# Three feed-forward stages: up products in Strassen's form, with the activations kept in DRAM

## The reference, cut to what matters

```python
# block 1 (FF = 4096) and block 3 (FF = 4096), with other names
m = rmsnorm(h, g) @ w_up            # (1024 x 1024) @ (1024 x 4096)
h = h + square(relu(m)) @ w_down    # (1024 x 4096) @ (4096 x 1024)
# block 2 (FF = 2816)
h = rmsnorm(x, g)
x = x + (silu(h @ w_gate) * (h @ w_up)) @ w_down
```

## Time and profile before

| | |
|---|---|
| median of 3 runs | 4399.23 us |
| span of the profiled execution (first to last instruction) | 4393.7 us |
| difference between the two | 5.5 us |
| TensorE busy (matmul) | 3927.2 us, 89% |
| VectorE busy | 2089.7 us, 48% |
| ScalarE busy | 1119.0 us, 25% |
| GpSimd busy | 869.4 us, 20% |
| DMA, mean | 73 GB/s, 319.75 MB |

### The profile page before, as it was taken

The page is one execution under the profiler, slowest core; times in us unless marked ns, Lnnn a source line. Parts: engine busy times, 40 slices in busy tenths (PEclk is TensorE's granted clock), DMA queues, the critical chain, the costliest instruction groups (busy, mean ns, idle before and its releaser), DMA issues. The chain is left out here.

```text
span 4393.7 us, 47463 instructions
## 1 busy us (share of the span) xinstructions
PE 3927.2 (89%) x18690; PEld 3275.1 (75%) x18690; DVE 2089.7 (48%) x2012; ACT 1119.0 (25%) x1368; POOL 869.4 (20%) x653
## 2 busy tenths in 40 slices
PE   9965999999989986767999999999943979999997
PEld 8953888888878776655888888878733958888886
DVE  3677445254544556365331322444768545253353
ACT  2503200000222233244211111243154552000001
POOL 1110222222222210200222222222220512222221
PEclk9987999999999998878999999999967989999998
DMA  3310111111133322442111111122272531111111
GB/s 131 103 45 23 46 51 49 48 48 48 48 130 110 117 80 46 120 156 67 46 50 48 48 48 48 48 82 91 88 177 39 158 126 48 48 48 48 48 50 60
DMA packets 446784, 319.75 MB, mean 73 GB/s; under 512 B 100181, under 2 KB 411989, under 8 KB 446649
## 3 DMA queue, kind: packets, MB, share of 16 engines
q1 hardware_dynamic: 437288, 283.72, 22.0%
q10 hardware_dynamic: 9360, 34.21, 2.0%
HBM read 245.22 MB, written 72.66 MB: 72 GB/s over the span
## 5 line engine op out<-in xcount | busy, mean ns | idle before, releaser
L191 POOL TENSOR_TENSOR c_wlo<-c_raw,c_whi 128x1024 fp32r<-128x1024 f32 (+1 forms) x169 | 409.4, 2423 | 1457.9 <-ACT c_whi L185 1457.9
L220 PE MATMUL c_acc<-c_hi,c_whi 128*128 128x512 f32 x1616 | 633.6, 392 | 0.6 <-POOL c_wlo L191 0.6
L221 PE MATMUL c_acc<-c_lo,c_whi 128*128 128x512 f32 x1616 | 629.2, 389 | 0.0
L222 PE MATMUL c_acc<-c_hi,c_wlo 128*128 128x512 f32 x1616 | 629.2, 389 | 0.0
L191 POOL TENSOR_TENSOR w_wlo<-w_raw,w_whi 128x1024 fp32r<-128x1024 f32 x116 | 291.6, 2514 | 1163.6 <-ACT w_whi L185 1163.6
L220 PE MATMUL c_acc<-pair,c_whi 128*128 128x512 f32 x1120 | 438.1, 391 | 45.6 <-POOL c_wlo L191 45.6
L185 ACT ACTIVATE c_whi<-c_raw 128x1024 fp32r<-128x1024 f32 (+1 forms) x169 | 177.1, 1048 | 1112.5 <-PE c_acc L222 1109.3
L221 PE MATMUL c_acc<-pair,c_whi 128*128 128x512 f32 x1120 | 437.5, 391 | 0.0
L222 PE MATMUL c_acc<-pair,c_wlo 128*128 128x512 f32 x1120 | 437.4, 391 | 0.0
L220 PE MATMUL c_acc<-c_hi,w_whi 128*128 128x512 f32 x1024 | 405.5, 396 | 12.4 <-POOL w_wlo L191 12.4
L221 PE MATMUL c_acc<-c_lo,w_whi 128*128 128x512 f32 x1024 | 399.7, 390 | 0.0
(11 more groups left out here) (592 smaller groups left out, 5858.7 us busy)
## 6 DMA issues: line engine op xcount, KB each, us to landing
c_raw<-in_w_ff SPq DMA_DIRECT2D x64, 512.0 KB, 4.0
proj<-c_tot ACTq DMA_DIRECT2D x49, 512.0 KB, 2.6
w_raw<-in_w_in SPq DMA_DIRECT2D x48, 512.0 KB, 4.4
c_raw<-in_w_gu SPq DMA_DIRECT2D x44, 512.0 KB, 3.8
w_raw<-in_w_mlp_up SPq DMA_DIRECT2D x32, 512.0 KB, 4.0
w_raw<-in_w_mlp_down SPq DMA_DIRECT2D x32, 512.0 KB, 4.0
h<-proj SPq DMA_DIRECT2D x25, 512.0 KB, 5.7
c_raw<-in_w_in SPq DMA_DIRECT2D x25, 512.0 KB, 4.0
```

The costliest lines, as they stand in the source:

```text
L191: pool.tensor_tensor(s.wlo[b][:, 0:kt, :], raw[:, 0:kt, :], s.whi[b][:, 0:kt, :].bitcast(F32), ALU.subtract).then_inc(s.lo[b], 1)
L220: pe.matmul(out, s.whi[b][:, k, :], x_hi, start=(k == 0), stop=False)
L221: pe.matmul(out, s.whi[b][:, k, :], x_lo, start=False, stop=False)
L222: mm = pe.matmul(out, s.wlo[b][:, k, :], x_hi, start=False, stop=(k == kt - 1))
```

## The change

Each pair of up tiles (256 columns of `w_up`; in block 2 one gate tile and one up tile) is seen as a 2x2 block product and computed in the form of Strassen and Winograd: the token axis is cut in two halves, the 256 columns in two, and the inner dimension in even and odd k (4 each). The pair takes seven products of half size, each 4 (k) x 3 = 12 matmuls of 512 columns, in place of eight.

- The sums of weights are made by GpSimd (`sums`: four operations of 512 elements per pair). The lower parts of the weights are made by VectorE (`split` there: three of 1024 elements, one of 512), the upper ones by ScalarE.
- The sums of activations are made once per stage: `E` for products 0 to 3, and `u4`, `u5` for 4 to 6. Some are made while the projection still runs, the others while the first pair does.
- Products 0, 3 and 6 accumulate in the same bank. ScalarE copies what is in PSUM to SBUF between them (`taken`), and VectorE adds (`add`).
- The weights of a pair come as one 1 MB load with rows of 1 KB. It is issued when all products of the pair before last are done (`sp.wait_ge(s["product"], NP * n)`).
- All up products of a stage come first. Each activation tile goes to DRAM (512 KB), from SP's queue, and comes back for the down products, where ScalarE and VectorE split it. The down products run in five groups of (2, 6, 8, 8, 8) tiles in blocks 1 and 3, and of (2, 6, 6, 4, 4) in block 2. GpSimd keeps the splits of the down weights.
- The loops are written out, and a stage has some 35 semaphores more.

The core of the diff (`act` is ScalarE, `dve` VectorE, `pool` GpSimd, `pe` TensorE, `sp` the SP queue):

```diff
+def product(pe, s, b, it, hi, lo, T, kt, middle=None, halves_of=None, rows_of=None, passed=None):
...
+        if rows_of is not None:
+            pe.wait_ge(s["x_lo"], rows_of + k + 1)
...
+PRODUCTS = ((0, True, 1), (2, True, 2), (1, True, 1), (0, False, 2), (2, False, 3), (3, True, 3), (0, False, 4))
+NP, QK, HALF_T = len(PRODUCTS), KD // 2, SEQ // 2
...
+    groups = []
+    for n, kt in enumerate(sizes):
+        at = sum(sizes[:n])
+        groups.append((u if n in (0, 1, 3) else x, at if n == 1 else 0, kt, at))
+    tiles = KD * len(groups)
+    total = outs + tiles // 2
...
+                def weights(n):
+                    b = buf(n)
+                    sp.dma_start(raw[b][:, :, :], up[:, :, n * 2 * P:(n + 1) * 2 * P]).then_inc(s[f"w_in{b}"], 16)
...
+                def row(f, X, r):
+                    if f >= 4:
+                        sp.wait_ge(s[f"x_in{f % 4}"], 16 * (f // 4))
+                    sp.dma_start(lands[X is u][:, r, :], put[f, :, :]).then_inc(s[f"x_in{f % 4}"], 16)
...
+                sp.wait_ge(s["u_lo23"], QK)
+                sp.wait_ge(s["u_lo56"], 2)
+                weights(1)
+                for n in range(M):
+                    if n:
+                        sp.wait_ge(s["product"], NP * n)
+                        if n < M - 1:
+                            weights(n + 1)
+                        else:
+                            for q in range(2):
+                                sp.dma_start(first_raw[q][:, 0:sizes[0], :], down[:, 0:sizes[0], q * P:q * P + P])\
+                                    .then_inc(s.landed[q], 16)
+                        if gated:
+                            put_gated(n - 1)
+                        else:
+                            put_second(n - 1)
+                    if n == M - 1:
+                        sp.wait_ge(s["product"], NP * n + 4)
+                        for f in range(sizes[0]):
+                            row(f, u, f)
+                    if not gated:
+                        put_first(n)
+                for f in range(sizes[0], sizes[0] + sizes[1]):
+                    row(f, u, f)
+                if gated:
+                    put_gated(M - 1)
+                else:
+                    put_second(M - 1)
+                sp.wait_ge(s["product"], NP * M)
+                for n, (X, r0, kt, f0) in enumerate(groups):
+                    for t in range(KD):
+                        q = KD * n + t
+                        if q >= 2:
+                            load_tile(sp, s, q % 2, outs + q // 2, down[:, f0:f0 + kt, t * P:t * P + P], kt)
...
+                def split(n, part):
+                    b = buf(n)
+                    act.wait_ge(s["w_sum"], 4 * n + 4)
+                    if n:
+                        act.wait_ge(s["product"], NP * (n - 1) + (3, 4, 6, 7)[part])
+                    elif part < 2:
+                        act.wait_ge(s.done[0], outs + 1)
+                    elif part == 2:
+                        act.wait_ge(s["m_summed"], 1)
+                    else:
+                        act.wait_ge(s.done[1], outs + 1)
+                    to, src = ((hi_a[:, :, :], raw[b][:, :, 0:P]), (hi_s, es[b][:, :, :, :]),
+                               (hi_b[:, :, :], raw[b][:, :, P:2 * P]), (hi_3, e3[b][:, :, :]))[part]
+                    copy(to, src, "w_hi")
...
+                def taken(n, part):
+                    p, to, src = ((0, y0[:, first_half], 0), (1, y1[n % 2][:, second_half], 2),
+                                  (3, y0[:, second_half], 0), (5, y1[n % 2][:, first_half], 3))[part]
+                    act.wait_ge(s["product"], NP * n + p + 1)
+                    if part == 0 and n:
+                        if gated:
+                            act.wait_ge(s["scaled1"], n)
+                        else:
+                            act.wait_ge(s["put0"], 16 * n)
+                    if part == 1 and n > 1:
+                        act.wait_ge(s[f"put1{n % 2}"], 16 * (n // 2))
+                    copy(to, s.psum[:, 4 * (n % 2) + src, :], "copied")
...
+                gained(3)
+                split(0, 0)
+                split(0, 1)
+                hi01(3)
+                square(6)
+                gained_again(0)
+                hi4(0)
+                hi56(0)
+                hi2(3)
+                square(7)
+                hi3(3)
+                hi4(1)
+                gained_again(1)
+                taken(0, 0)
+                hi4(2)
+                hi4(3)
+                taken(0, 1)
+                gained_again(2)
+                split(0, 2)
+                hi56(1)
+                hi56(2)
+                gained_again(3)
+                taken(0, 2)
+                hi56(3)
+                split(0, 3)
+                split(1, 0)
+                split(1, 1)
+                act.wait_ge(s["n_eps"], 1)
+                act.wait_ge(s["m_summed"], 1)
+                act.activation(halves(inv), s.psum[:, 6:8, :], ACT.Ln, scale=1.0 / D, bias=c.low[:, 0:1])\
+                   .then_inc(s["m_logged"], 1)
+                act.wait_ge(s["m_logged"], 1)
+                act.activation(inv, inv, ACT.Exp, scale=-0.5).then_inc(s["m_root"], 1)
+                taken(0, 3)
...
+                for n in range(1, M):
+                    last = n == M - 1
+                    split(n, 3)
+                    shaped_second(n - 1)
+                    taken(n, 0)
+                    taken(n, 1)
+                    if not last:
+                        split(n + 1, 0)
+                    else:
+                        act.wait_ge(s["product"], NP * n + 3)
+                        split_down(0)
+                    taken(n, 2)
+                    if not last:
+                        split(n + 1, 1)
+                    else:
+                        act.wait_ge(s["product"], NP * n + 4)
+                        split_down(1)
+                    shaped_first(n)
+                    taken(n, 3)
+                    if not last:
+                        split(n + 1, 2)
+                for f in range(sizes[0]):
+                    upper(f, u, f)
+                shaped_second(M - 1)
+                for n, (X, r0, kt, f0) in enumerate(groups):
+                    final = n == len(groups) - 1
+                    for t in range(KD):
+                        q = KD * n + t
+                        if n == 0 and t < sizes[1]:
+                            upper(sizes[0] + t, u, sizes[0] + t)
+                        if q + 2 < tiles:
...
+                def sums(n):
+                    b = buf(n)
+                    first_in, second_in = (raw[b][:, 0::2, 0:P], raw[b][:, 1::2, 0:P])
+                    first_out, second_out = (raw[b][:, 0::2, P:2 * P], raw[b][:, 1::2, P:2 * P])
+                    s1, s2, s3 = es[b][:, 0, :, :], es[b][:, 1, :, :], e3[b][:, :, :]
+                    pool.wait_ge(s[f"w_in{b}"], 16 * (n // 2 + 1))
+                    if n == 1:
+                        pool.wait_ge(s.done[1], outs + 1)
+                    pool.tensor_tensor(s1, first_out, second_out, ALU.add).then_inc(s["w_sum"], 1)
+                    pool.tensor_tensor(s3, first_in, first_out, ALU.subtract).then_inc(s["w_sum"], 1)
+                    pool.wait_ge(s["w_sum"], 4 * n + 1)
+                    pool.tensor_tensor(s2, s1, first_in, ALU.subtract).then_inc(s["w_sum"], 1)
+                    pool.wait_ge(s["w_sum"], 4 * n + 3)
+                    pool.tensor_tensor(first_out, second_in, s2, ALU.subtract).then_inc(s["w_sum"], 1)
...
+                def halved(n, p):
+                    bank, begins, part = PRODUCTS[p]
+                    pe.wait_ge(s["w_lo"], 4 * n + part)
+                    if p == 0 and n < 2:
+                        pe.wait_ge(s.free[n], outs + 1)
+                    if p == 0 and n == 1:
+                        pe.wait_ge(s["m_logged"], 1)
+                    if p == 0 and n > 1:
+                        pe.wait_ge(s["added"], 3 * n - 3)
+                    if p == 3:
+                        pe.wait_ge(s["copied"], 4 * n + 1)
+                    if p == 4:
+                        pe.wait_ge(s["copied"], 4 * n + 2)
+                    if p == 6:
+                        pe.wait_ge(s["copied"], 4 * n + 3)
+                    out = s.psum[:, 4 * (n % 2) + bank, :]
+                    for k in range(QK):
+                        if n == 0:
+                            pe.wait_ge(s[("u_lo01", "u_lo01", "u_lo23", "u_lo23", "u_lo4", "u_lo56", "u_lo56")[p]], k + 1)
+                        w_hi, w_lo = weight(buf(n), p, k)
+                        x_hi, x_lo = moving(p, k)
+                        pe.matmul(out, w_hi, x_hi, start=begins and k == 0, stop=False, skip_group_check=not begins)
+                        pe.matmul(out, w_hi, x_lo, start=False, stop=False, skip_group_check=not begins)
+                        mm = pe.matmul(out, w_lo, x_hi, start=False, stop=k == QK - 1, skip_group_check=not begins)
+                    mm.then_inc(s["product"], 1)
```

(94 more changed lines are left out.)

440 lines of the change are left out of this document (274 added, 166 removed).

## The result

The changed kernel takes 4480.97 us (median, 4478.67 to 4485.62) against 4399.81 us in the same session: a ratio of 1.0187, interval [1.0173, 1.0202]. It is 1.9% slower. The prediction, 4374 us with a range of 4322 to 4445, was wrong in sign and in range. The profiled execution has a span of 4480.3 us, 86.6 us above the 4393.7 of before.

The account below looks back on a forecast made before the run. TensorE was taken to bound the feed-forward stages, so only fewer matmuls could shorten them. 146.9 - 51 - 25.5 - 21 - 21 - 3 = 25 us of gain, from 4399.2 to 4374 us, with a range of 4322 to 4445.

Parts of the forecast that it names:

- the saving: Up products: 12 matmuls fewer in each of 54 pairs, 2.72 us per pair, 146.9 us in all.
- the pairs stay hidden: Rival for the steady pairs: their two terms are near 0, a gain of 67 us, 4332 us; chance 0.28.
- L: Steady pairs: landing time of a pair's 1 MB weight load, taken as 5.5 us.
- late weights: Rival for the steady pairs: the 1 MB load lands in 8.0 us, 95 us more, 4469 us; chance 0.19.
- start: First pairs of each stage: TensorE waits for sums and weights, 17 us per stage, 51 in all (36 to 66).
- entry: Entry to the down products: late weights of the third tile, first tile and lost clock, 25.5 us in all (12 to 36).
- So a pair takes 19.04 to 20.4; I take 19.8: Steady pairs of blocks 1 and 3: 0.75 us over the matmuls' 19.04 in each of 28 pairs, 21 us.
- The ring: Steady pairs, blocks 1 and 3: closed chain of load, sums, splits, square, put_first and next load, 18.95 us against 19.04.
- The rest ... 3 us: Block 2's last down group with short tiles, and more semaphores to clear: 3 us (0 to 8).
- one costs 0.2267 us: Feed-forward stages: 48 matmuls take 10.88 us, so each matmul costs 0.2267 us.
- a step other than 0.227 us: Sign that the prediction is wrong: matmuls inside a product not 0.227 us apart; no price given.
- the rival on half products: Rival: each of 378 product starts costs TensorE a gap; at 0.1 us each 38 us, 4412 us; chance 0.08.

Follow-up runs that it names:

- e9: e6 with other gaps between its buffers, so that all feed-forward weights and streamed operands begin at a remainder of 160 over 256; 4337.32 us, ratio 0.9864.
- e6: e5 with all eight first rows of activations asked for when product 4 of the last pair is done; 4343.57 us, ratio 0.9872.
- e1: The changed kernel with ScalarE's norm step (tail_scalar) taken two turns earlier in the last down group; 4387.10 us, ratio 0.9969.
- e5: e1 with gaps of 64 and 96 bytes that bring feed-forward weights and streamed operands to one remainder over 128; 4348.70 us, ratio 0.9882.
- e10: e9 with VectorE's residual(7), early23(3) and total_of(7) ahead of the first two weight splits and differences, and ScalarE's hi56(0) after hi3(3); 4347.15 us, ratio 0.9887.
- e4: The kernel before the change with 192 unused bytes ahead of c.hi in SBUF, nothing else; 4421.85 us, ratio 1.0048.

## Why the prediction was wrong

**Right: what bounds the kernel, and the saving.** 54 pairs lost 12 matmuls each. e9, with the two missed causes taken away (and e6's 5 us at the entry), is 62 us faster than before; that lies beside the rival "the pairs stay hidden" (67 us).

**Right: the load.** L was put at 5.5 us; the landings of the kernel after (columns as in the earlier trace rows) are 5.3 to 5.6 in blocks 1 and 3:

```profile
ff_raw1f<-in_w_mlp_up SPq DMA_DIRECT2D x8, 1024.0 KB, 5.6
ff_raw0f<-in_w_mlp_up SPq DMA_DIRECT2D x8, 1024.0 KB, 5.3
...
ff_raw1f<-in_w_ff SPq DMA_DIRECT2D x8, 1024.0 KB, 5.5
ff_raw0f<-in_w_ff SPq DMA_DIRECT2D x8, 1024.0 KB, 5.5
```

In block 2 the buffer whose landing the page gives has 5.1. The 8.0 us of the "late weights" rival, worked out there from two loads of 512 KB one after the other, is not borne out. That rival gave 4469, near the measured 4481, by a mechanism that did not take place: a time that comes out near is no proof of its reason.

**Right in the sum: start and entry.** The start was put at 51 us and cost 50, the entry at 25.5 and cost 28. In the start the waits stood where they were put, with other sizes. TensorE at the start of block 1, kernel after:

```profile
517.77 1.98 PE L950 MATMUL c_acc<-c_tot,ones 128*128 128x512 f32 x4 [3.07 <-DVE c_tot L983]
...
527.01 0.50 PE L937 MATMUL c_acc<-pair,ff_hi_b 128*128 128x512 f32 x1 [1.71 <-DVE ff_raw1r L1030]
...
535.72 0.50 PE L937 MATMUL c_acc<-pair,ff_hi_b 128*128 128x512 f32 x1 [3.58 <-DVE pair L1020]
```

3.1 us ahead of the sums for 4.9 predicted. Pair 1 began 33.7 us after the first product, as computed, and ended at 54.4 for 56.0; in blocks 2 and 3 it ended at 60.2 and 55.5. Its product 3 waited 0.8, 5.7 and 0.8 us in the three blocks for 3.2 predicted, so in part errors cancel in the 50.

At the entry the sum came out, but the account in the prediction is only part of the cause. It counted the rows and the last write as work of the DMA queue; e6 took the rows away and gained 5 us. The rest is the wait of `put_second` for the last square, with the load behind it.

**Wrong, on the safe side: "So a pair takes 19.04 to 20.4; I take 19.8".** The steady pairs had no wait. The ring was put at 18.95 us, and I then added half of what the lock (VectorE and GpSimd slower side by side, as in the earlier trace rows) and the write could cost. The write is issued 2 us before the weights (658.49 and 660.53 in the order of time) and so is mostly out of the way, VectorE's last split ends 1.8 us before the first sum starts (664.15 and 665.90), and instructions that follow each other directly on an engine start about 0.1 us closer than their durations say (1.06 us at 1163.76 on ScalarE, the next at 1164.72): the chain from the sums to `put_first` takes 6.8 us, not the 7.9 that I added up. With the gate, the chain from the sums to `scaled1` takes 13.1 us for 14.5 (2410.16 to 2423.24), and the two multiplies end 1.05 us before the next sums start. The multiplies take 1.23 us each and the sums 1.29 there: no run shows the up to 2.3 and 1.2 us that the prediction took for the lock with the gate. 42 us were priced and 0 paid, and in e9, where the pairs take 19.04 us, still nothing.

**Wrong, and decisive: "The rest ... 3 us".** I looked at the last group only as an amount of work (5 us on VectorE per tile of 5.4 us) and never followed its order, as I had done for the start. The diff shows `split_down(q + 2)` ahead of `tail_scalar(t - 2)`, and `tail_vector(t)` between two additions to h. Before the change `tail_scalar(t - 2)` also stood behind a split, but behind that of tile t, which waits for product t - 2; now that of tile t + 2 is ahead of it, and waits for product t. This term was 102 us for 3; e1 gave 94 of them back. It alone turns the forecast's sign.

**Wrong: "one costs 0.2267 us".** Of every matmul left, I kept the price of before. The prediction named a step other than 0.227 us as a thing that would make it wrong, yet gave it no price and no chance; the rival on half products asked for gaps at their starts, and none appeared. The step changed to 230 to 234 ns because buffers had moved, also outside the three stages (GpSimd's splits in the following projection came 11.20 us apart for 10.88). 48 us by the account; the runs took back 38 (e5 against e1) and 6 (e9 against e6).

Together: 25 us of gain forecast, + 42 not paid, - 99 for the last group, - 48 for the step and - 8 for the entry and the small tiles of block 2 gives -88, for the -86.6 of the traces.

## What to carry to other kernels

Follow the order of every engine at each end of a changed stretch, the last group as well as the first: a step that is covered by its amount of work can still stand behind a wait for the very product that it should run beside. The same holds for a DMA queue, where a load can stand behind a write that waits for another engine. When a change moves buffers, compare the matmul count of an unbroken stretch before and after; if it drops with no wait, as here from 884 to 868 in 200 us, compare the remainders of the weights' and the streamed operand's addresses over 256. Before moving a step earlier in an engine's queue, see what it waits for: whatever stands behind it waits too, as the two splits of e10 did for 3.24 us.

## What the runs showed of the hardware

- The step between matmuls of 128x128 by 512 columns in fp32r depends on where weights and streamed operand lie in SBUF relative to each other. One remainder over 256: 227 ns in all rows. Differing ones: up to 236 ns, most often 233 to 234. The engine's busy share is 100% and its granted clock 1.00 in both cases (868 matmuls in 200 us in the kernel after, 884 in e9). It was worth 48 us here, 1.1% of the time, and 22 us in the kernel before by a gap of 192 bytes (e4). No run here has a stream of such matmuls without its weight loads, so whether these are behind the longer step is not shown. What is shown is that the place of the two operands relative to each other sets the step.
- The four waits in block 1's last group, of 5.9 to 8.2 us, cost more than themselves: the tile behind each had a mean granted clock of 0.78 to 0.87 and took 12.5 to 13.9 us for 10.88. The waits were 31 us and the slow tiles 8.5 us more.
- A 1 MB load with rows of 1 KB lands in 5.1 to 5.6 us (medians). Four loads with rows of 256 bytes in its place, 256 KB each, land 4.4 to 4.9 us after their own issue (median of each group).
